# Modulation products taken from one stage and given to two others, with three steps of the norms put elsewhere

## What is computed

```python
for l in range(DEPTH):                                   # DEPTH = 2
    mod = (s_lat @ w_ada[l] + b_ada[l])[:, None, :]      # 1024 x 6144: shifts, scales, gates
    mod_c = s_ctx @ w_ada[l] + b_ada[l]                  # the same weights for the context
    h = modulate(rmsnorm(x, norm1_g[l]), sh1, sc1)
    hc = modulate(rmsnorm(xc, norm1_g[l]), csh1, csc1)
    p = h @ w_in[l]                                      # GLU | q, k, v | gates
    ...                                                  # k_c, v_c from hc; rope on q and k
    y_conv = conv_branch(p[..., :GLU_END], ...)          # a * sigmoid(g), 31-tap depthwise conv
    y_attn = merge_heads(neighbourhood_attention(q, k, v, k_c, v_c, na_rpb[l])) @ w_na_out[l]
    x = x + g1 * gated_merge(p[..., QKV_END:], y_conv, y_attn, w_out[l])
    h2 = modulate(rmsnorm(x, norm2_g[l]), sh2, sc2)
    x = x + g2 * conv_ffn(h2, w_up[l], ffn_dw[l], ffn_dw_b[l], w_down[l])
    # the context goes through the same layer while l == 0
```

## Time and profile before

| what | value |
|---|---|
| profiled execution, whole | 2357.61 us |
| its span, first instruction to last | 2355.9 us |
| mean granted TensorE clock | 0.977 |
| TensorE busy (matmuls) | 2234.9 us, 95% |
| VectorE busy | 1853.5 us, 79% |
| ScalarE busy | 1319.6 us, 56% |
| DMA | 499.82 MB, mean 212 GB/s |
| chain that ended last | PE 69%, DVE 16%, ACT 6%, DMA 5%, issue 4% |

### The profile page before, as it was taken

How to read it: one execution, slowest core, us unless ns; L and a number is a source line. 1 busy time by engine, 2 the same in 40 slices (tenths; PEclk the granted TensorE clock), 3 DMA queues, 4 the chain that set the end, 5 groups by cost and what they waited for, 6 DMA issues and landing times.

```text
span 2355.9 us, 49810 instructions
## 1 busy us (share of the span) xinstructions
PE 2234.9 (95%) x18210; PEld 2155.7 (92%) x18210; DVE 1853.5 (79%) x3258; ACT 1319.6 (56%) x2140; POOL 119.9 (5%) x231
## 2 busy tenths in 40 slices
PE   7899999998989999799999999999999999989998
PEld 5798899998889999789999999998999999979998
DVE  4796867789789977987998878867877877878655
ACT  4366655546766555476664644646644644676443
POOL 0100000000000100000000001000001001000000
PEclk8999999999999999999999999999999999999999
DMA  8746676754348775434687677671678687735654
GB/s 346 241 156 206 224 238 212 247 179 148 121 153 275 271 240 188 143 126 149 215 273 261 225 276 267 215 251 60 228 271 274 211 287 261 236 120 166 231 166 131
DMA packets 150407, 499.82 MB, mean 212 GB/s; under 512 B 17392, under 2 KB 21616, under 8 KB 148720
## 3 DMA queue, kind: packets, MB, share of 16 engines
q1 hardware_dynamic: 113360, 374.01, 45.9%
q0 software_dynamic: 32544, 119.55, 16.2%
q10 hardware_dynamic: 4352, 4.20, 0.6%
HBM read 496.65 MB, written 1.05 MB: 211 GB/s over the span
## 4 chain that ended last, share of the span: by engine, by line
PE 69%; DVE 16%; ACT 6%; DMA 5%; issue 4%; ACTq 0%; DVEq 0%; SPq 0%; POOLq 0%; POOL 0%
PE bank_pair L1811 21%; PE bank_pair L1812 20%; PE bank_pair L1813 20%; DVE w_lo L1099 4%; DMA modraw<-in_w_mod 3%; DVE arena L1379 3%; ACT w_hi L588 2%; PE ps_o L1824 1%; DVE h_lo L1260 1%; DVE small L1454 1%; ACT arena L816 1%; DVE arena L1630 1%; PE bank_pair L2197 0%; DMA e_plain<-in_w_mod 0%; PE ps_o L2182 0%
## 5 line engine op out<-in xcount | busy, mean ns | idle before, releaser
L1099 DVE TENSOR_TENSOR w_lo<-raw,w_hi 128x1024 fp32r<-128x1024 f32 (+2 forms) x764 | 840.7, 1116 | 216.0 <-ACT w_hi L588 212.3
L588 ACT ACTIVATE w_hi<-raw 128x1024 fp32r<-128x1024 f32 (+2 forms) x764 | 729.6, 968 | 408.0 <-PE bank_pair L1813 288.4
L1811 PE MATMUL bank_pair<-h_hi,w_hi 128*128 128x256 f32 x3056 | 879.5, 288 | 16.4 <-DVE w_lo L1099 9.1
L1812 PE MATMUL bank_pair<-h_lo,w_hi 128*128 128x256 f32 x3056 | 869.1, 284 | 0.0
L1813 PE MATMUL bank_pair<-h_hi,w_lo 128*128 128x256 f32 x3056 | 868.7, 284 | 0.0
L1811 PEld LDWEIGHTS bank_pair<-h_hi,w_hi 128*128 128x128 f32 x3056 | 590.5, 193 | 38.9 <-issue 26.9
L1811 PE MATMUL bank_pair<-e_both,w_hi 128*128 128x256 f32 (+1 forms) x2064 | 595.0, 288 | 26.7 <-DVE e_both L1747 13.1
L1812 PEld LDWEIGHTS bank_pair<-h_lo,w_hi 128*128 128x128 f32 x3056 | 591.0, 193 | 0.3
L1813 PEld LDWEIGHTS bank_pair<-h_hi,w_lo 128*128 128x128 f32 x3056 | 590.8, 193 | 0.0
L1812 PE MATMUL bank_pair<-e_both,w_hi 128*128 128x256 f32 (+1 forms) x2064 | 588.6, 285 | 0.0
L1813 PE MATMUL bank_pair<-e_both,w_lo 128*128 128x256 f32 (+1 forms) x2064 | 588.4, 285 | 0.0
(11 more groups left out here) (257 smaller groups left out, 2080.7 us busy)
## 6 DMA issues: line engine op xcount, KB each, us to landing
modraw<-in_w_mod POOLq DMA_DIRECT2D x224, 512.0 KB, 5.1
raw<-in_w_gu SPq DMA_DIRECT2D x176, 512.0 KB, 4.4
raw<-in_w_up SPq DMA_DIRECT2D x132, 512.0 KB, 5.2
raw<-in_w_gate SPq DMA_DIRECT2D x48, 512.0 KB, 3.7
raw<-in_w_dn SPq DMA_DIRECT2D x64, 384.0 KB, 4.6
raw<-in_w_dn SPq DMA_DIRECT2D x64, 320.0 KB, 3.7
raw<-in_w_down SPq DMA_DIRECT2D x48, 384.0 KB, 5.1
raw<-in_w_down SPq DMA_DIRECT2D x48, 320.0 KB, 5.0
```

The lines of the kernel that those rows point to most:

```text
L588: nc.scalar.activation(w_hi[:, p, HALF * f:HALF * f + w], raw[:, p, HALF * f:HALF * f + w], ACT.Copy)\
L1099: nc.vector.tensor_tensor(w_lo[:, p, at], raw[:, p, HALF * f:HALF * f + w], w_hi[:, p, at].bitcast(F32), ALU.subtract).then_inc(lo_ready, 1)
L1811: nc.tensor.matmul(out, l[0], r[0], start=start, stop=False)
L1812: nc.tensor.matmul(out, l[0], r[1], start=False, stop=False)
```

## The change

There are four edits.

1. The `glu` stage of x, in both layers, has `mods=2` instead of 1: blocks 33 to 36 (before: 37 and 38) in layer 0, and 51 to 54 (before: 53 and 54) in layer 1.
2. Part 0 of the context's `down` has no products any more (before: blocks 33 to 36).
3. Slot 3 of the norm of x for layer 1 goes from the second slab of the context's `q` stage to the first slab of its `v` stage, and slot 5 from the first to the second slab of `v`.
4. In a `down` with a norm ahead, the slots 6 and 7 stand behind the slab's addition to the residual (`add_product`), as the slots 0 to 5 do.

```diff
@@ layer_a
-        stage("glu", a[f"w_glu{l}"], SLAB, 2, mods=1)
+        stage("glu", a[f"w_glu{l}"], SLAB, 2, mods=1 if early else 2)
@@ layer_a, "down"
-                  mods=int(part == 0),
+                  mods=int(x == "x" and part == 0),
@@ the walk through the plan
-                        q.ahead, q.slots = s, {0: (0, 1, 2), 1: (3,)}
-                        s1.ahead, s1.slots = s, {0: (4, 5), 1: (6, 7)}
+                        q.ahead, q.slots = s, {0: (0, 1, 2), 1: ()}
+                        s1.ahead, s1.slots = s, {0: (3, 4), 1: (5, 6, 7)}
@@ do_down on VectorE
-                        if s.ahead is not None and j >= 6:
-
-                            norm_ahead(s, j)
                         add_product(s, j, j, p, 0)
-                        if s.ahead is not None and j < 6:
+                        if s.ahead is not None:
                             norm_ahead(s, j)
```

## The result

Four runs of the changed kernel have a median of 2370.59 us (2370.09 to 2372.32), four of the kernel before 2356.02 us (2355.66 to 2357.61). The ratio of the two is 1.0057, with a 95% interval of 1.0039 to 1.0075: slower by 14.6 us, between 9.2 and 17.7. The forecast was 2368.3 us, in a range of 2359 to 2375.5 us. The four runs of the changed kernel lie closer together than such runs usually do: all 25 single runs of the changed kernel on record go from 2362.57 to 2376.78 us, with a median of 2370.31.

What follows compares the result with a forecast made beforehand. VectorE was taken to set the pace in rope and convolution behind x's `glu`, TensorE normally elsewhere. +14.6 - 0.5 - 2.0 = +12.1 us on the median of 2356.16 gave 2368.3 us, range 2359 to 2375.5 us.

Steps and rivals of the forecast that it cites:

- What bounds the kernel where: Rope and convolution after x's `glu`: VectorE sets the pace, so any delay of its first rope instruction reaches the end.
- Edit 1, the work: x's `glu`: four more parts, 4.6 us per layer, hide in VectorE's idle time and push rope by nothing.
- Edit 1, the data: x's `glu`: `modraw` rounds of 7.8 us exceed a 5.76 us slab; rope 7.3 us later per layer, +14.6 us.
- the rival of quiet landings: x's `glu`: stalls slow the weights too, rounds take 6.1 us; +1.9 us, 2358.1 us; chance 0.11.
- The rule that was weighed against this: Loads in `glu`: 2.0 us plus bytes over 436 GB/s, 3.2 us for 512 KB, round 5.5 us, no cost.
- The first rival: x's `glu`: loads land within 3.5 us, no product waits, only gains stay; 2353.7 us; chance 0.07.
- Edit 2: Context's `down`: without products, TensorE's 0.5 us wait for the norm's sums goes; -0.5 us, bounds 0 and -0.8.
- Edit 3: Layer 1's norm of x: TensorE's 2.99 us wait and slow clock go, but the norm is late; gain 2.0 us.
- The rival of the norm as the new bound: Layer 1's `glu`: norm chain 3 us longer than counted turns the gain into 1 us loss; 2371.3 us; chance 0.09.
- Edit 4: x's `down`: low parts of slab 8 move 0.4 us, covered by 3.8 us of high parts; zero.
- The sum: Whole kernel: +14.6 - 0.5 - 2.0 = +12.1 us, giving 2368.3 us; chance 0.73.
- The signs that were named: Profile after: `modraw` waits some 3 us, rounds 7 to 9 us, rope 28 us behind first product, norm waits moved.

Runs made afterwards that it cites:

- edits 1 and 2 alone: Kernel before with two products per slab in x's `glu` and none in the context's `down`, norms unchanged: 2372.28 us against 2357.35, ratio 1.0057.
- layer 0 alone: Kernel before with two products per slab only in layer 0's `glu` of x, context's `down` keeping its products: 2362.27 us against 2357.49, ratio 1.0020.
- the early blocks: Changed kernel with blocks 35 and 53 loaded long ahead into a place of their own: 2360.75 us, ratio 1.0018, +4.2 us.
- light loads: Changed kernel with loads of blocks 34 to 36 and 52 to 54 cut to 64 KB per part instead of 512: 2359.04 us, ratio 0.9998.
- edit 3 alone: Kernel before with only slots 3 and 5 of layer 1's norm of x moved: 2357.04 us against 2357.35, ratio 0.9999.
- edit 4 alone: Kernel before with only slots 6 and 7 put behind the slab's addition: 2357.18 us, ratio 0.9995.
- the late sum with the scaling cut: Kernel before with TensorE's norm sum behind its slab's second half and slot 5 moved to `v`'s second slab: 2350.42 us against 2356.14, ratio 0.9981.
- the late sum: Kernel before with only TensorE's norm sum moved behind the second half of its slab in one-body stages: 2356.30 us against 2357.49, ratio 0.9989.

## Why the prediction was right

**What bounds the kernel where.** Right. The delay of VectorE's first rope instruction was passed on: it is 5.70 us late at rope of layer 0 and 5.69 us late at 600 us; 6.58 us more come at rope of layer 1, and nothing of it is given back. The idle time behind the last product, 2.13 us, shows in the runs with two products per slab: less the 1.15 us of the second product, 0.98 us are left of it, and rope is late by VectorE's waits less 0.98 us. With edits 1 and 2 alone 6.5 and 6.8 us of waits make 5.5 and 5.8, as measured; in the changed kernel 7.1 and 7.5 make 6.1 and 6.5, where 6.23 and 6.57 were measured; with layer 0 alone 7.8 make 6.8, as measured; with the early blocks 3.2 make 2.2, where 22.63 - 20.68 = 1.95 was measured.

**Edit 1, the work.** Right: with light loads the eight products pushed rope by 0.0 us in layer 1, and by 0.7 in layer 0 with 1.94 us of waiting for data still there.

**Edit 1, the data.** The mechanism is right and the size a little too large. The rounds were taken as 7.8 us; they were 7.45 us in the mean of layer 0 and 7.56 in that of layer 1. Two layers cost 6.24 + 6.58 = 12.8 us instead of 14.6. The landing was sized well: 7.8 - 1.87 - 0.4 = 5.5 us, and the six landings of the table above are 5.5 us in the mean. The way from product to issue was right too (1.87 or 1.88 us in all six). The term that was off is the last one, 0.4 us from landing to the next start: it was 0.1 us in five of the six rounds and 0.5 in one. It had been worked out by taking the median landing of both parts, 6.3 us, from rounds of c = 1; the loads of c = 1 in those rounds took 6.3, 6.6 and 6.6 us, which leaves 0.2. The bound of 6.1 us a round rested on a load of SyncE's queue (3.8 us); the shortest landing among the six is 3.8 us as well.

The last rounds of layer 1, 6.56 and 5.81 us, come near the 6.1 us of the rival of quiet landings; but the first one took 10.31 us. A late landing was followed by short ones in both layers, as the feedback of this rival would have it, and the mean of three rounds hid that: the forecast was helped here by averaging and not by a right account of each round.

The rule that was weighed against this (the Trainium skill, "DMA: Bandwidth & Descriptors", the anatomy of one DMA on the SWDGE path: 2.0 us plus bytes over 436 GB/s) would have had every load in time. The medians of the traces don't agree with it at either size here: 5.0 us for 512 KB, where an estimate by the rule is 3.2, and 2.8 us for 64 KB, where it is 2.15. The shortest loads of the two stages in layer 0 came near it, 3.5 us (the one issued at 477.43) and 2.2 us. The first rival's own condition, a landing within 3.5 us, did hold up: with light loads the one landing of 5.0 us made VectorE wait 1.75 us, and no other wait was above 0.42.

**Edit 2.** Wrong in its size, and in its reason. Half a microsecond was forecast, from a wait of 0.5 us for the sum of the norm that the products were thought to cause. The wait is 0.4 us after, and also 0.4 in the traces of edit 3 alone and edit 4 alone, which have the products. From the first matmul of the context's `down`, part 0, to the first of layer 0's `glu` it is 61.64 us before and 61.67 after. So edit 2 gave nothing. In the ledger its place has -1.29 us, which is something else: a slow clock that this one run didn't have. TensorE waits 2.44 us ahead of layer 0's `glu` before and 2.46 after; before, the granted clock in the four microseconds behind it was 0.67, after, 1.00:

```profile
466.00:470.00 4.00, 4.00 (x25) 4.00 (x25) 3.89 (x9) 0.12 (x1) 0.00 (x0) 0.67 0.68 228
```

```profile
467.00:471.00 4.00, 4.00 (x36) 4.00 (x35) 3.86 (x9) 0.00 (x0) 0.00 (x0) 1.00 0.71 246
```

25 matmuls against 36 are started in the same time, and the slab takes 7.00 us against 5.71.

**Edit 3.** Right in its mechanism: the wait for L1269 went, the norm became late in its place, and a part of the gain was kept. 2.0 us were forecast, 1.46 came (1.45 by itself). The start was met: 27.29 us behind the start of the context's `q`, where the forecast's 901.7 makes 27.2. What was off is the slab itself. The prediction let it end 0.8 us behind the last low part, with a slow clock "included", some 6.7 us in all; it took 7.19 us, and of that the clock is some 1.1. In the time of the whole kernel this can't be seen (0.9988 to 1.0009). The rival of the norm as the new bound would have lost 1 us, and no trace shows that: TensorE does wait for the norm, but less than it did.

**Edit 4.** Zero, as forecast, with the cover that was named.

**The sum.** By the places that the edits touch, +12.8 + 0.0 - 1.5 = +11.3 us, against 12.1 forecast. The profiled run has 14.6. The other 3.3 us are the rest of the ledger: 0.75 ahead of any edit, -1.3 of clock, and 3.8 in small steps from 657 to 810 us and behind rope of layer 1. I did not find a place for the last ones. The run with edits 1 and 2 alone gave +13.4 with an interval from 9.4 to 17.4, so the medians can't say whether they belong to the change. That stays open. That the measured +14.6 is also the forecast's term for edit 1 is chance: the ledger gives that edit 12.8.

**The signs that were named.** The waits for `modraw`, rope some 28 us behind the first product (26.9), its delay passed on, and no wait for L1269 all came. Four signs did not come as named. The waits ahead of the later pairs were 3.3, 1.9 and 1.9 us in layer 0 and 5.2, 1.6 and 0.7 in layer 1, not some 3 each. Three of the six rounds were shorter than 7 us and one longer than 9; one, of 5.81, was under the 6 us that would have spoken against the forecast, which it could be without doing so, since the sum of three rounds decides. The wait for the norm's sum in the context's `down` stayed. And the wait ahead of layer 1's `glu` was 2.12 us, a little above the 1 to 2 named.

## What to carry to other kernels

Before more is asked of a buffer with one place, work out its round trip (use to issue, landing under the load of that very stage, landing to use) and hold it against the time between two uses; a period of 11.5 us hid what one of 5.8 us could not, with the same bytes in all. One block per layer loaded early gave back some 10 of the 14.6 us. And when the wait for a sum is taken away, look at what comes next in the same chain: moving TensorE's sum alone and moving the root with it (edit 3) both let `glu` start 2.9 us sooner, since it then waited for the splits; only with the scaling cut in two as well did that wait go, and the time fell by 4.5 us. A median over both parts (here 6.3 us) should not be subtracted from the rounds of one of them.

## What the runs showed of the hardware

After a wait of 2 to 3 us TensorE's clock sometimes goes to half speed for some microseconds and sometimes not, in the same place of the same stage: 0.67 before and 1.00 after, behind 2.44 and 2.46 us ahead of layer 0's `glu`. There six of the ten traces of this case have the slow clock (before, edits 1 and 2, edit 3, edit 4, layer 0 alone, and the late sum with the scaling cut) and four don't. Ahead of layer 1's `glu` it was 0.57 behind 2.11 us (edit 3 alone), 1.00 behind 2.13 us (the early blocks) and 1.00 behind 1.77 us (the late sum). It costs 1.3 to 1.5 us each time (a slab of 7.0 to 7.2 us instead of 5.7), about as much as many an edit here is worth.

Single runs of one kernel spread over 15 us, and the granted clock goes with it. Of the 71 runs of the kernel before beside the experiments, the five with a mean granted clock of 0.975 took 2363.0 us in the mean, and the nine with 0.980 took 2354.2. Whether the slow stretches are the whole of the spread isn't shown.

In the changed kernel's two `glu` stages a product that waited for its load started 0.1 us after the landing (0.5 once), and the next load was issued 1.87 to 1.89 us after the product's start. The landing itself, of 512 KB with the weights moving beside it, lay between 3.5 and 8.3 us there.
